# Mixed chunk's gathered values: one multiplication or four, gathers over 128 rows or 220

## What is computed

```python
def one_chunk(args):
    xb, ib, gb = args
    act = jax.nn.gelu(jnp.einsum('cd,ced->ce', xb, u_tab[ib]), approximate=False)
    return jnp.einsum('ce,ced->cd', gb * act, v_tab[ib])
return lax.map(one_chunk, (xc, idx, g)).reshape(B, S, D)
...
ffn = peer_ffn(x, peer_wq[l], peer_k1[l], peer_k2[l], peer_u[l], peer_v[l])
x = layer_norm(ALPHA * x + ffn, ln2_g[l], ln2_b[l])
```

## Times and profile before

| | us |
|---|---|
| Median of 3 runs | 3563.76 |
| Lowest and highest | 3557.1, 3574.85 |
| The profiled execution, its device time | 3557.03 |
| Span of the profiled execution (first to last instruction) | 3555.2 |

### The profile page before, as it was taken

The page is one execution under the profiler, slowest core; times in us unless marked ns, Lnnn a source line. Parts: engine busy times, 40 slices in busy tenths (PEclk is TensorE's granted clock), DMA queues, the critical chain, the costliest instruction groups (busy, mean ns, idle before and its releaser), DMA issues.

```text
span 3555.2 us, 40390 instructions
## 1 busy us (share of the span) xinstructions
PE 3118.1 (88%) x14161; PEld 1724.8 (49%) x14161; DVE 2569.1 (72%) x5029; ACT 884.5 (25%) x2173; POOL 1611.7 (45%) x1321
## 2 busy tenths in 40 slices
PE   7488879997899996884999998999999999998970
PEld 5467635674566664442444443444434444333430
DVE  5755529987767876886888986768858864556689
ACT  6354211113233331200111562736601000000000
POOL 5500000114666544444444444344336677777563
PEclk9788989998999998897999999999999999999985
DMA  8478632446889979977689999899999999999996
GB/s 276 132 260 329 263 118 90 136 149 215 302 294 319 318 250 336 371 288 299 244 325 351 332 316 372 310 375 348 339 399 366 407 370 356 342 342 368 408 410 250
DMA packets 313258, 1073.17 MB, mean 302 GB/s; under 512 B 36704, under 2 KB 62944, under 8 KB 309216
## 3 DMA queue, kind: packets, MB, share of 16 engines
q0 software_dynamic: 170704, 606.75, 46.8%
q1 hardware_dynamic: 101904, 363.16, 27.6%
q10 hardware_dynamic: 40448, 100.68, 7.7%
HBM read 931.52 MB, written 138.94 MB: 301 GB/s over the span
## 4 chain that ended last, share of the span: by engine, by line
DMA 16%; POOL 13%; PE 12%; DVE 8%; issue 5%; DVEq 1%; ACT 0%; ACTq 0%
DMA rows<-v,expert_ids 9%; PE ps L1807 7%; POOL rows L134 5%; POOL hidden_sums L1772 4%; DMA rows<-u,expert_ids 4%; POOL turned_rows L134 3%; DMA turned_rows<-v,expert_ids 3%; DVE row_sums L169 2%; DMA turned_rows<-u,expert_ids 1%; DVE rows L163 1%; PE ps L108 1%; PE ps L110 1%; PE ps L109 1%; PE ps L1825 1%; PE ps L1826 0%
## 5 line engine op out<-in xcount | busy, mean ns | idle before, releaser
L134 POOL DMA_INDIRECT rows<-u,expert_ids x477 | 588.8, 1234 | 780.4 <-DVE hidden_sums L163 641.7
L1807 PE MATMUL ps<-turned_rows,mixer_state 128*128 128x512 f32 x2048 | 894.8, 595 | 9.3 <-DMA mixer_state<-u_t 8.6
L134 POOL DMA_INDIRECT rows<-v,expert_ids x527 | 603.4, 1145 | 572.4 <-DVE row_sums L169 436.6
L169 DVE SCALAR_TENSOR_TENSOR row_sums<-rows,hidden_sums,row_sums 128x1024 f32<-128x1024 f32 x518 | 657.1, 1281 | 271.1 <-DMA rows<-v,expert_ids 266.2
L1844 PE MATMUL ps<-shared_64k 128*128 128x512 f32 x1536 | 670.2, 599 | 25.2 <-DVE shared_64k L1975 24.3
L1807 PEld LDWEIGHTS ps<-turned_rows,mixer_state 128*128 128x128 f32 x2048 | 385.4, 191 | 479.1 <-issue 463.9
L1844 PEld LDWEIGHTS ps<-shared_64k 128*128 128x128 f32 x1536 | 294.4, 192 | 401.0 <-issue 401.0
L163 DVE CUSTOM_DVE_ANT_0 rows<-rows,x_first 128x1024 f32<-128x1024 f32 x256 | 307.1, 1219 | 63.1 <-DMA rows<-u,expert_ids 60.4
L163 DVE CUSTOM_DVE_ANT_0 rows<-rows,branches 128x1024 f32<-128x1024 f32 x221 | 268.3, 1217 | 80.2 <-DMA rows<-u,expert_ids 77.9
L108 PE MATMUL ps<-x_hi_t_b,shared_64k 128*128 128x384 f16 x912 | 303.3, 333 | 18.3 <-DMA shared_64k<-w_pairs_kept 17.5
L109 PE MATMUL ps<-x_lo_t_b,shared_64k 128*128 128x384 f16 x912 | 303.0, 332 | 0.0
(11 more groups left out here) (529 smaller groups left out, 4968.9 us busy)
## 6 DMA issues: line engine op xcount, KB each, us to landing
mixer_state<-u_t ACTq DMA_DIRECT2D x128, 512.0 KB, 7.2
shared_64k<-v SPq DMA_DIRECT2D x128, 512.0 KB, 7.0
rows<-strips SPq DMA_DIRECT2D x32, 768.0 KB, 7.2
h_kept<-branches ACTq DMA_DIRECT2D x32, 768.0 KB, 10.6
shared_64k<-weights_kept SPq DMA_DIRECT2D x32, 768.0 KB, 9.4
shared_64k<-h_kept SPq DMA_DIRECT2D x32, 768.0 KB, 13.2
shared_64k<-s_pairs_kept SPq DMA_DIRECT2D x32, 512.0 KB, 7.2
rows<-w_t SPq DMA_DIRECT2D x30, 512.0 KB, 5.5
```

What stands on the lines that cost most here:

```text
L134: nc.gpsimd.indirect_dma_start(row_tile(M, n), None, A["u" if r < NSEL else "v"], bass.IndirectOffsetOnAxis(ap=M["idx"][:, c, e:e + 1], ax ...
L169: nc.vector.scalar_tensor_tensor(acc[:, e % 2, :], src, hid[:, c % 2, e:e + 1], acc[:, e % 2, :], ALU.mult, ALU.add).then_inc(used, 1)
L1807: m = pe.matmul(ps[:, 4 + u % 4, 0:UT], uk[u % 4][:, k, :], x1t[:, k, :], start=k == 0, stop=k == KD - 1)
```

## The change

The loop that issues the small gathers no longer takes one per row for 128 rows. `VALUE_AT` spreads them evenly over rows 869 to 1086: value e goes ahead of row 869 + e*219//128 (NROW - 2*PART - VALUES_FROM = 219). The values of the first part are thus issued with rows 869 to 922, of the second with 923 to 976, of the third with 978 to 1031, of the fourth with 1033 to 1086. On VectorE the one wait and the one 128x128 multiplication ahead of row 1024 become four, ahead of rows 1024, 1056, 1088 and 1120. Each waits for its 32 values (and all before them) and multiplies 32 columns, with a drain behind it. Nothing else moves: number, size and queue of all transfers are the same.

```diff
+PART = 32
...
-        if r == NSEL:
-            if c == HYB:
-                dve.wait_ge(M["values_in"], 16 * NSEL)
-            else:
-                dve.wait_ge(M["hid_gelu"], c + 1)
+        if c == HYB and e % PART == 0:
+            dve.wait_ge(M["values_in"], 16 * (e + PART))
+            part = slice(e, e + PART)
+            nc.vector.tensor_tensor(hid[:, c % 2, part], hid[:, c % 2, part], gg[:, c, part], ALU.mult)
+            dve.drain()
+        elif r == NSEL:
+            dve.wait_ge(M["hid_gelu"], c + 1)
             nc.vector.tensor_tensor(hid[:, c % 2, :], hid[:, c % 2, :], gg[:, c, :], ALU.mult)
             dve.drain()
...
+VALUE_AT = {}
+for _e in range(NSEL):
+    VALUE_AT.setdefault(VALUES_FROM + (_e * (NROW - 2 * PART - VALUES_FROM)) // NSEL, []).append(_e)
...
         for n in range(R_MERGE + NR, NROW):
-            if n >= VALUES_FROM:
-                gather_values(n - VALUES_FROM)
+            for e in VALUE_AT.get(n, ()):
+                gather_values(e)
             if n == LATE_FROM:
                 pool.wait_ge(h_mm, NBLK)
             gather_rows(nc, pool, M, A, n, n + 1)
```

More of the change, by code:

```diff
@@ L1770, in gather_values @@
                     pool.wait_ge(side_st[i], 16 * (NBLK // 4))
-            if e < NSEL:
+            if 0 <= e < NSEL:
                 nc.gpsimd.indirect_dma_start(
```

## The result

The median went from 3560.43 us (3552.03 to 3574.85, 6 runs) to 3523.18 us (3512.93 to 3534.19, 6 runs): ratio 0.9898, 95% interval 0.9874 to 0.9923, that is 27 to 45 us less. The forecast was 21.6 us less. The profiled execution took 3512.93 us, with a span of 3511.1.

What follows compares the result with a forecast made beforehand. GpSimd's issue was taken to bound 2863.7 to 3235.5, the DMA engines 3235.5 to 3402.1, then three engines level. Terms -26.4 + 4 + 0.8 = -21.6 us give 3542 from the median 3563.76 (3535 profiled), range 3524 to 3565.

Steps and rivals of the forecast that it cites:

- Product 31: The TensorE product ahead of row 1067, ending the stretch from the first small gather: forecast to come 26.4 us earlier.
- the DMA price of 508 us: First small gather to product 31: DMA engines last, needing 508 us in place of 538.4, at 0.22 us per small gather.
- TensorE's floor: Rival, chance 0.12: up to product 31 TensorE's groups set the limit, 45 us earlier; 40 us gained in all, 3524.
- GpSimd's price: First small gather to product 31: 327 instructions at 1.485 us each, 486 us.
- The dearer price of the saturated stretch: Same 327 GpSimd instructions at the 1.567 us measured from 3235.5 to 3402.1: 512 us.
- the slower rival: Rival, chance 0.07: GpSimd stays last up to product 31 at 1.71 us an issue, 558 us; +25 us, 3588.
- The loss between two servers: Up to product 31: DMA engines and GpSimd, at 96% of them, lose 4 us to each other.
- The last stage: Behind product 31: seven small gathers moved there add 4 us (1.5 to 9.0), multiplications 0.8 us.
- The multiplications: VectorE: four quarter-width multiplications in place of one add 0.8 us, at most 1.1, two of them behind product 31.
- the covered waits: VectorE's four waits for values cost nothing; nearest cover 34 rows, 55 us with GpSimd's lead, against landing of 9.2 us.
- What would show it: Signs up to product 31: share 1.02 to 1.03, some 400 GB/s, buffer waits a few us each, landing 12 to 18 us.
- the likeliest case: The forecast's own case, chance 0.57: DMA engines last up to product 31; 21.6 us gained, range 3529 to 3554.

Runs made afterwards that it cites:

- the other two profiles: The changed kernel itself, unaltered, timed and profiled twice more: ratios to the kernel before 0.9921 and 0.9916, sums 775.9 and 780.6 us.
- the parts alone: Kernel before with only its one multiplication split into four, small gathers still one per row over rows 869 to 996: 3552.42 us, ratio 0.9987.

## Why the prediction was right or wrong

Direction and cause were right: one stretch was bound by GpSimd's issues and the next had time to spare on GpSimd, and the spread fills that time, so that the waits for buffers that stood behind row 996 are gone. The size was too small, 21.6 us against about 30 by the stage and 37 by the medians. Two terms of the sum were off, by 16 to 20 us and by 5 to 12 us, in opposite directions. That they partly cancel, and so leave the sum near the measured time, is luck.

- **Product 31.** Forecast 26.4 us earlier, counted from the first small gather; measured 44.8, 45.9 and 42.7 (538.4 to 493.6, 492.5, 495.7). The step that failed is the DMA price of 508 us. It charged each small gather 0.22 us of the DMA engines, got by turning the share's distance to 1.03 into unused time. In the changed kernel 394 GB/s x 493.6 us = 194.5 MB, at 408 GB/s 477 us, so, with 408 taken for the full rate, the 119 small gathers and all else had 17 us, 0.14 us each at most. The DMA engines could do it in the time that TensorE needed. What decided was the rival "TensorE's floor", which had 0.12: it said 45 us, and the first stage is 612.6 to 614.5 us in five profiles of three kernels, with GpSimd busy for 229 to 396 us of it. The prediction's own floor, 3357 or 611 us after 2746, was within 2 to 4 us, but the sum put the DMA engines above it by a price that no row carried.
- **GpSimd's price** was near. Forecast 327 issues at 1.485, 486 us; measured 323 at 1.524, 492, and 1.45 and 1.52 in the other two profiles. The dearer price of the saturated stretch, 1.567, was too high, and the slower rival's 1.71 did not come. Its reason was half right. In the changed kernel 84 issues up to product 31 were longer than 1.4 us, and only 20 of them overlap a product. But of the issues in whose first 0.93 us VectorE ran nothing none was longer than 0.98 us, in any of the thirteen profiles. So the long ones do go with VectorE's work, that on the rows included, and not with full DMA queues alone; what makes some long and others not is open.
- **The loss between two servers**, 4 us, was not seen: the floor left none.
- **The last stage.** Forecast 4.8 us more; measured 16.4, 10.1 and 13.7. The text read this stage off two late rows: "the last rows go at 1.28 us" and "VectorE works without a gap". Over the whole stage the kernel before took 107.3 us for 77 issues, 1.39 each, and VectorE waited 8.6 us for rows. The upper bound, 9.0, was too low. It counted seven small gathers' issues, and forgot that GpSimd, bound up to product 31, begins the last stage with the ring not full. By the timelines it had issued row 1074 when product 31 began in the profile of before, and row 1071 in that of after, with nine small gathers to come. So 89 issues are left in place of 77. Three of the 12 more are rows and nine are small gathers; at 1.39 us each (124 us for 89) they are 16.7 us. The other two profiles agree: 83 and 87 issues left, 6 and 10 more, for 10.1 and 13.7 us. The text had it that lateness is not made up there, and then did not count how late GpSimd would start.
- **The multiplications**, 0.8 us, and the covered waits were right: the multiplication shown above follows its row without a gap, and the parts alone cost nothing measurable. One distance was misread: the third wait stands 57 rows behind its last value (1031 to 1088), not over 80, which still covers it.
- **What would show it.** Share 1.02 came as forecast, the GB/s (394) nearly. GpSimd's waits for buffers did not appear (1.2 us); rows landed after a median of 10.5 us, not 12 to 18:

```profile
DMA to landing us min/median/max: 6.1/10.5/14.9
```

Both are signs of a GpSimd that is still level with the others, where the forecast had it at 96%. And the forecast named gaps of more than 9 us on VectorE in the last stage as the sign that it is wrong. They came: 23.6 us in place of 8.6, 15.0 more, and 17.7 and 20.9 in the other two profiles. By its own sign the account of the last stage was wrong.

The measured time against before, 0.9898, lies inside the range, at its low end. The 37 us of the medians are just beyond the likeliest case's own range of 10 to 35, the 27 to 33 of the sums inside it, but by another path: TensorE's floor less a dear last stage, not the DMA engines' price.

## What to carry to other kernels

When one queue issues two kinds of work and is bound in one stage and waits in the next, spreading the second kind over both gains the waits at most; look for the next floor (here the reload of a three-deep buffer behind TensorE) and price it as the rival that it is. Count a stage's start state as well as its instructions: each row that the ring lacks at the start cost here as much as an instruction moved. A price that no row carries, such as the DMA cost of small packets worked out from a share, should be the wide end of a range and not the middle of a sum.

## What the runs showed of the hardware

- An indirect gather of 128 single 4-byte elements cost GpSimd what a gather of 128 rows of 4 KB cost it (0.93 to 0.95 us for the shortest of either, with 0.30 us behind it), and the DMA engines about 0.14 us at most, an estimate from 394 GB/s over 493.6 us with 408 GB/s as the full rate.
- GpSimd's issues took 0.94 us on average, and never over 0.98, when VectorE ran nothing in their first 0.93 us, in all thirteen profiles. Beside a tensor_tensor of 128x1536 they took 1.42 to 1.59 us on average, leaving out the kernel without small gathers, where four overlap; beside three scalar_tensor_tensor of 128x512 over the same data 1.13 and 1.16, about what they took beside the rows' own scalar_tensor_tensor (1.15 to 1.22 in the profiles with all small gathers). The Trainium skill (SBUF — State Buffer, section "SBUF: two separate sides") names an exclusive lock on a shared port pair as what makes GpSimd wait; that issues beside an idle VectorE were never long agrees with it. The runs also show less waiting beside the second version of the product; whether its form or its three shorter instructions did that was not separated, and both versions read two operands from SBUF.
- Identical programs reached the start of the dense v side anywhere between 2727.8 and 2754.9 us. A gain of under 1% is read better from a stage's own length than from the total.
